# Building the expert gates of a two-layer trunk on one core: VectorE makes every one-hot part, and all gates pass through HBM

## The reference, cut to what matters

```python
def fourier_mix(u):                      # 4 groups of 256 channels, real part of a 2-D transform
    f = jnp.fft.fft2(ug, axes=(1, 3), norm='ortho').real

def peer_ffn(h, w_pq, sub_keys, peer_u, peer_v):
    q = (hf @ w_pq).reshape(T, PEER_HEADS, 2, PEER_KEY_DIM)
    s = jnp.einsum('thpd,hpnd->thpn', q, sub_keys)
    s1, i1 = lax.top_k(s[:, :, 0], PEER_TOPK)          # 16 of 128 first keys
    s2, i2 = lax.top_k(s[:, :, 1], PEER_TOPK)          # 16 of 128 second keys
    cand_s = s1[..., :, None] + s2[..., None, :]
    cand_i = i1[..., :, None] * PEER_KEYS + i2[..., None, :]
    top_s, pos = lax.top_k(cand_s, PEER_TOPK)          # 16 pairs per head and token
    gate = jax.nn.softmax(top_s, axis=-1)
    ...
    a = jnp.einsum('tkd,td->tk', ub, xb)               # ub: the chosen rows of peer_u
    a = jax.nn.gelu(a, approximate=False) * gb
    return jnp.einsum('tk,tkd->td', a, vb)             # vb: the chosen rows of peer_v
```

## Time and profile before

| what | before |
|---|---|
| median of 3 runs (lowest to highest) | 4188.33 us (4185.52 to 4189.72) |
| the profiled execution, its own time | 4193.56 us |
| its span, first to last instruction | 4191.4 us |
| busy share PE, PEld, DVE, ACT, POOL | 91%, 82%, 49%, 34%, 31% |
| mean granted TensorE clock | 0.937 |
| HBM read, written | 510.65 MB, 37.22 MB |

### The profile page before, as it was taken

One profiled execution on the slowest core, in us unless ns is written; L12 is line 12 of the kernel. 1 busy time (PEld: TensorE's weight loads), 2 busy tenths in 40 slices (PEclk: granted clock), 3 DMA queues, 4 the chain that ended last, 5 costly groups with the idle time before them and its releaser, 6 DMA issues.

```text
span 4191.4 us, 63927 instructions
## 1 busy us (share of the span) xinstructions
PE 3794.0 (91%) x20274; PEld 3456.9 (82%) x20274; DVE 2036.4 (49%) x3928; ACT 1409.3 (34%) x2015; POOL 1307.9 (31%) x585
## 2 busy tenths in 40 slices
PE   4999898966699999999989999998666999999998
PEld 4999798966678888898979987898666788888887
DVE  6586436965555222222246954479555632222223
ACT  2334323422233333333333342333222333333333
POOL 1332133543322222222213221345333222222222
PEclk8999999977789999999999999999677999999999
DMA  5486132322134444444436841333220444444442
GB/s 204 161 252 209 56 111 86 111 81 100 65 113 149 139 143 137 142 140 142 135 117 198 252 158 53 116 96 110 101 100 23 154 144 140 142 138 142 141 141 97
DMA packets 204743, 549.05 MB, mean 131 GB/s; under 512 B 17136, under 2 KB 87152, under 8 KB 202608
## 3 DMA queue, kind: packets, MB, share of 16 engines
q1 hardware_dynamic: 128016, 465.88, 34.3%
q10 hardware_dynamic: 76640, 82.06, 5.7%
HBM read 510.65 MB, written 37.22 MB: 131 GB/s over the span
## 4 chain that ended last, share of the span: by engine, by line
PE 83%; DVE 6%; issue 5%; POOL 2%; ACT 2%; DVEq 1%; DMA 0%; POOLq 0%; ACTq 0%; SPq 0%
PE bank L671 26%; PE bank L449 17%; PE bank L450 16%; PE bank L451 16%; PE bank L649 5%; DVE hot L1505 2%; POOL split_lo L360 1%; POOL hot L1112 1%; PE bank L542 1%; ACT split_hi L355 1%; PE bank L563 1%; PE bank L467 0%; PE bank L438 0%; PE bank L596 0%; DVE raw L376 0%
## 5 line engine op out<-in xcount | busy, mean ns | idle before, releaser
L360 POOL TENSOR_TENSOR split_lo<-raw,split_hi 128x1024 fp32r<-128x1024 f32 x436 | 1068.4, 2451 | 2637.3 <-ACT split_hi L355 2637.3
L449 PE MATMUL bank<-h_hi,split_hi 128*128 128x384 f32 x3712 | 1276.3, 344 | 84.9 <-DVE h_lo L1169 63.1
L355 ACT ACTIVATE split_hi<-raw 128x1024 fp32r<-128x1024 f32 x768 | 813.9, 1060 | 1490.4 <-PE bank L451 1202.8
L450 PE MATMUL bank<-h_lo,split_hi 128*128 128x384 f32 x3712 | 1259.7, 339 | 0.0
L451 PE MATMUL bank<-h_hi,split_lo 128*128 128x384 f32 x3712 | 1258.2, 339 | 0.0
L360 DVE TENSOR_TENSOR split_lo<-raw,split_hi 128x1024 fp32r<-128x1024 f32 x332 | 411.9, 1241 | 1341.9 <-ACT split_hi L355 1341.5
L449 PEld LDWEIGHTS bank<-h_hi,split_hi 128*128 128x128 f32 x3712 | 711.3, 192 | 121.0 <-DVE h_lo L1169 78.1
L450 PEld LDWEIGHTS bank<-h_lo,split_hi 128*128 128x128 f32 x3712 | 712.5, 192 | 7.8
L451 PEld LDWEIGHTS bank<-h_hi,split_lo 128*128 128x128 f32 x3712 | 710.2, 191 | 0.0
L671 PE MATMUL bank<-split_hi,a_hi 128*128 128x512 f32 x1536 | 490.8, 401 | 6.0 <-DVE a_lo L1530 5.8
L649 PE MATMUL bank<-hot,hot 128*128 128x128 bf16 x2304 | 284.5, 297 | 224.4 <-POOL hot L1112 131.4
(11 more groups left out here) (167 smaller groups left out, 2852.3 us busy)
## 6 DMA issues: line engine op xcount, KB each, us to landing
raw<-panels SPq DMA_DIRECT2D x768, 512.0 KB, 3.3
mod_raw<-mod_panels SPq DMA_DIRECT2D x96, 512.0 KB, 4.4
gates_spilled<-kept ACTq DMA_DIRECT2D x8, 4096.0 KB, 11.4
spilled<-gates_spilled ACTq DMA_DIRECT2D x128, 256.0 KB, 3.8
raw<-mod_panels SPq DMA_DIRECT2D x16, 512.0 KB, 4.5
bias<-bias_in ACTq DMA_DIRECT2D x16, 256.0 KB, 2.7
dft<-dft_in ACTq DMA_DIRECT2D x2, 1152.0 KB, 8.7
silu_c<-c_in ACTq DMA_DIRECT2D x2, 1024.0 KB, 5.1
```

What stands on the lines that cost most here:

```text
L355: nc.scalar.activation(col(split_hi, s % 2, D), col(raw, s, D), ACT.Copy).then_inc(hi_ready[s], 1)
L360: eng.tensor_tensor(col(split_lo, s % 2, D), col(raw, s, D), col(split_hi, s % 2, D).bitcast(F32), ALU.subtract).then_inc(lo_ready[s], 1)
L449: mm(out, w_hi, col(rhs_hi, kk, n), start=(kk == 0), stop=False)
L450: mm(out, w_hi, col(rhs_lo, kk, n), start=False, stop=False)
```

## The change

VectorE now makes everything for the gate matmuls, for one tile of 4 tokens at a time, in a ring of four buffers: `keys_hot` writes both one-hots with one instruction of 1024 elements, one tile ahead, and `gated_hot` all three gated parts with one of 1536. POOL has no work in the gate stage until its end; the `split_lo` of the panels there moves to DVE, one after each four tiles. The gate stage has 6 groups instead of 3: one score panel, then 4 tiles (16 tokens) instead of 8. One more group of 4 score panels (FINAL_G) runs behind it, so 52 score panels run ahead of the outputs instead of 36, and 52 output panels run in a row. A chunk is 32 tokens; all 12 chunks are stored to HBM, and the gates come back for four panels j at a time (12 x 128 x 128 values, 768 KB). DVE then gates a panel with one instruction. In the Fourier step the channel table keeps 129 cosine and 127 sine columns and two zero columns (258 instead of 512); the second half of the channels is taken from the same columns with the sine tables negated, and the rows of `w_four_out` are reordered on the host to match.

```diff
-BATCH = 2 * TILE_T
-NB = T // BATCH
-CHUNK_T = 64
+CHUNK_T = 32
-SPILLED = CHUNKS - KEPT
+HOTS = 4
+HOT = (2 + PARTS) * TILE_T * P
+BLOCK = 4
-ALONE_G, WITH_G = 6, 3
-EARLY_G = ALONE_G + WITH_G
+ALONE_G, WITH_G, FINAL_G = 6, 6, 1
+EARLY_G = ALONE_G + WITH_G + FINAL_G
...
-            def one_hots(n, b):
-                dve.wait_ge(gate_mm, l * NT + 2 * n + 2)
-                dve.wait_ge(hot1_pool, l * NB + n + 1)
...
+            def keys_hot(n, r):
+                dve.wait_ge(gate_mm, l * NT + n + 1)
+                shape = [P, 2, P, TILE_T]
+                V.tensor_tensor(hot_pair(r),
...
+                                ALU.is_equal).then_inc(eq_ready, 1)
+            def gated_hot(n, r):
+                dve.wait_ge(eq_ready, l * NT + n + 1)
+                shape = [P, PARTS, P, TILE_T]
+                V.tensor_tensor(hot_parts(r), hot_pair(r)[:, 0, :, :].unsqueeze(1).broadcast_to(shape),
...
+                                ALU.mult).then_inc(hot_ready, 1)
+            def hot_group(i, last=False):
+                for s in range(SLOTS):
+                    for r in range(PANEL_TILES):
+                        n = (i * SLOTS + s) * PANEL_TILES + r
+                        if not (last and s == SLOTS - 1 and r == PANEL_TILES - 1):
+                            keys_hot(n + 1, (r + 1) % HOTS)
+                        gated_hot(n, r)
+                    split_panel_lo(dve, *ahead(l * GROUPS + (FIRST["peer"] + ALONE_G) + i, s))
...
-            with pool.Fori(0, WITH_G) as i:
-                for s in range(SLOTS):
-                    split_panel_lo(pool, *ahead(peer + ALONE_G + i, s))
-                    for b in range(BATCHES):
-                        third_part((i * SLOTS + s) * BATCHES + b, b % 2)
+            for s in range(SLOTS):
+                split_panel_lo(pool, *ahead(peer + ALONE_G + WITH_G, s))
...
+            early_gelu(ALONE_G + WITH_G, 0)
+            early_gelu(ALONE_G + WITH_G, 1)
+            for b in range(KEPT):
+                act.wait_ge(gates_stored[b], (l + 1) * (CHUNKS // KEPT) * 16)
+            load_gates(0, 0)
+            load_gates(1, 1)
+            early_gelu(ALONE_G + WITH_G, 2)
+            early_gelu(ALONE_G + WITH_G, 3)
...
-                        last = mm(bank[4 + u % 2][:, :], col(f, 2 * g + c)[:, t * P:(t + 1) * P],
-                                  dft[:, DFT_CH + c * 512:DFT_CH + (c + 1) * 512], start=(c == 0), stop=(c == 1))
+                        last = mm(bank[4 + u % 2][:, 0:FC], col(f, 2 * g + c)[:, t * P:(t + 1) * P],
+                                  dft[:, DFT_CH + c * FC:DFT_CH + (c + 1) * FC], start=(c == 0), stop=(c == 1))
```

More of the change, by code:

```diff
@@ L554, in fourier_tokens @@
                     out = bank[6 + u % 2]
[L555 to L558, removed]
+                    cosines, sines = dt, HALF + 1 + dt
+                    for w0, which in ((cosines, 0), (sines, 1 + dt)):
+                        mm(out[:, 0:TP], yg[:, w0:w0 + P], dft[:, DFT_P + which * TP:DFT_P + (which + 1) * TP],
+                           start=(which == 0), stop=(which > 0))
                     for t in range(2):
-                        for part in range(2):
-                            w0 = (1 + t) * 512 + part * FD + dt * P
-                            r0 = DFT_S + (2 * t + part) * TS
+                        for w0, which in ((cosines, 0), (sines, 1 + dt)):
+                            w0 += (1 + t) * FC
+                            r0 = DFT_S + (3 * t + which) * TS
                             last = mm(out[:, TP:T], yg[:, w0:w0 + P], dft[:, r0:r0 + TS],
-                                      start=(t + part == 0), stop=(t + part == 2))
+                                      start=(t == 0 and which == 0), stop=(t == 1 and which > 0))
                     last.then_inc(y2_ready, 1)
@@ L634, in _, with build_gates @@
             route_tiles(TT - 1)
[L636 to L650, removed]
+            def build_gates(n, r):
+                pe.wait_ge(hot_ready, l * NT + n + 1)
+                pe.wait_ge(gate_copied, l * NT + n + 1)
+                keys2, parts = hot_pair(r), hot_parts(r)
+                for t in range(TILE_T):
+                    w = keys2[:, 1, :, t]
+                    o = col(bank[2 + r], t, P)
+                    for c in range(PARTS):
+                        last = mm(o, w, parts[:, c, :, t], start=(c == 0), stop=(c == PARTS - 1))
+                last.then_inc(gate_mm, 1)
             carry(pe)
@@ L996, in split_act, with pair @@
                 copy(col(a_hi, b), col(act_f, b)).then_inc(ahi_ready, 1)
-            def pair(i, p, load=True, last=False):
+            def pair(i, load=None, last=False):
                 g = peer + i
@@ L1005, in pair @@
                 split_act(2 * i + 1, 1, (g, 0))
-                if load:
-                    load_gates(i + 2, p)
+                if load is not None:
+                    load_gates(*load)
                 if not last:
@@ L1543, in _, with early_outputs @@
             carry(dve)
-            with dve.Fori(0, NB // 2) as i:
-                one_hots(2 * i, 0)
-                one_hots(2 * i + 1, 1)
-            def gated_early(i, s):
-                j = i * SLOTS + s
-                gated(j, s % 2, lambda at, n: gel_early[:, bass.ds(j * T + at, n)], s // 2, i)
-            def early_outputs(i, first=False):
+            keys_hot(0, 0)
+            with dve.Fori(0, WITH_G - 1) as i:
+                hot_group(i)
+            hot_group(WITH_G - 1, last=True)
+            def early_outputs(i, p, turn, first=False):
                 for s in range(SLOTS):
-                    gated_early(i, s)
+                    j = i * SLOTS + s
+                    gate_act(j, s % 2, s, gel_early[:, bass.ds(j * T, T)], p, turn)
                     if s % 2 == 0 and not (first and s == 0):
```

207 lines of the change are left out of this document (94 added, 113 removed).

## The result

The changed kernel takes 3926.83 us (median of 4 runs, 3925.07 to 3929.48) against 4188.06 us before (4185.52 to 4189.72): ratio 0.9377, 95% interval 0.9361 to 0.9394. The prediction was 3941 us, with 3905 to 4005 as its range. The profiled execution took 3925.07 us, its span is 3923.0 us, 268 us less than before. The medians lie 261 us apart; the profiled execution before was 5.5 us above its median.

The account below looks back on a forecast made before the run. PE bounds all long stretches except the gate stage, 305.4 us twice per launch, where it waits for POOL and DVE. 4193.56 - 228.4 (two layers) - 19 (Fourier) = 3946 us, 3941 with the median 5.2 us lower; range 3905 to 4005.

Parts of the forecast that it names:

- the clock term: Gate stage: panels lose a tenth of the 84 us that half clock would cost, 8 us per layer.
- First tile: Start of the gate stage: without POOL's split beside DVE, the first tile starts near 864.0 instead of 868.5 us.
- 24 periods: Gate stage: PE sets 24 periods of one panel and four tiles, 9.84 us each, less the first panel: 232.0 us.
- Rival A: Gate stage: the clock stays at half for the score panels, 84 us instead of 8 per layer, 4093 us; chance 0.09.
- Four last panels: End of the gate stage: four last score panels, each covered by POOL's split chain, take 17 us.
- Wait ahead of the outputs: From last score to first output: gelu, split, rounding and `a_lo` beside POOL's split make PE wait 4.3 us.
- Sixteen pair steps: Pairs: 16 pair steps of 8.40 us become output panels of 4.30 us in a row, 65.6 us less per layer.
- The Fourier term: Fourier step: 48 matmuls per layer shortened by 0.215 us each, 10.3 us; taken as 9.5, 19 us in all.
- C: Gate stage: hand-overs do not overlap, PE takes tiles at DVE's pace, period 11.5 us, 4021 us; chance 0.05.
- D: Gate stage: DVE's two-operand instructions keep their long form and bound it, period 22.4 us, 4546 us; chance 0.04.
- B: Gate stage: tile matmuls run faster once the clock is up, a tile taking 0.77 us, 3819 us; chance 0.04.

Follow-up runs that it names:

- x1_eight: Changed kernel with eight tiles behind each of 12 score panels instead of four behind each of 24, still 52 panels ahead of the outputs: 3930.70 us.
- x9_fewer_ahead: Changed kernel with eight tiles behind each of 12 score panels and 44 score panels ahead of the outputs instead of 52: 3925.53 us.
- x5_weights_flat: Changed kernel with the tile matmuls' weights read as 128 neighbouring elements instead of every fourth, giving other gates than the right ones: 3921.91 us.
- x6_both_flat: Changed kernel with tile matmuls' weights and gated parts both read as neighbouring elements, giving other gates than the right ones: 3821.14 us.
- x10_pairs: Changed kernel with gated parts laid out by token pairs, written in two instructions of 768 elements; TensorE's moving side steps 4 bytes, not 8: 3809.35 us.
- x3_pool_third: Changed kernel with only the third gate part of each tile back on POOL, the panels' splits staying on VectorE: 3931.96 us.

## Why the prediction was right

Every step held, and the forecast was 14 us high. The traces put it 21 us high, of which the clock term makes 16; every other term is off by 1.3 us a layer or less, steps 2 and 5 the other way. Seven of the 21 us came back by chance: the profiled execution after lies 1.8 us below its median, where I had counted with 5.2 us above.

1. *First tile.* 4.5 us per layer predicted, 5.3 found; the same three instructions, without POOL beside them.
2. *24 periods.* 232.0 predicted, 232.7 found. A panel with the hand-over behind it takes 4.28 us instead of 4.18, and four tiles 5.59 instead of 5.66, counted from first start to first start. The reading that PE would set the period, VectorE resting 2.5 us in it, held as it stands (2.77).
3. *Clock.* This term was the wrong size: 8 us were set aside, and none was lost in the periods: the granted clock is 0.99 over the stage and 1.00 from 862 to 1084 us. Rival A fell. By the rule that I cited from the Trainium skill (TensorE: Matmul & The Clock Gate, "A second HAM failure mode: psum-queue depth-cycling") a stage that goes round its PSUM banks with short idles would have swung between the two levels. This trace has the banks and the cycle without the idle time, and stays at 1.00 from period to period; x1_eight does so too.
4. *Four last panels.* 17 predicted, 16.8 found.
5. *Wait ahead of the outputs.* 4.3 predicted, 4.54 found, by the mechanism named.
6. *Sixteen pair steps.* 65.6 predicted, 66.9 found. The number is right and the step is still misleading: it reads as a gain of its own. The sixteen panels cost 12 x 4.28 + 16.8 = 68 us in steps 2 and 4, so the exchange is even, as x9_fewer_ahead shows. What paid was that PE no longer stands.

The Fourier term was taken a little under its upper end, 9.5 of 10.3; the trace gives 10.1. The loads from odd columns, which I could not price, cost nothing. Of the rivals, C (hand-overs that do not overlap) and D (long instructions on VectorE) are refuted by the rows of the period. B had the tile matmuls wrong in the same way as the forecast: both asked whether the clock sets their 0.118 us. It does not, and the weights hardly do (x5_weights_flat); x6_both_flat and x10_pairs show that the reading of the moving side did, so that over 100 us lay in a layout that the forecast took as given.

## What to carry to other kernels

When an engine's program has two jobs, look at which one stands in front: a job that waits for the slow chain delays a job that could have run, and moving the first away was worth 245 us in the changed kernel, while the speed of either was worth a few there. Count a panel that moves at both places before you call its removal a gain. And once TensorE sets a stage, ask of its matmuls how their operands lie in memory: time per matmul that does not follow the clock was a sign of it here.

## What the runs showed of the hardware

- 48 matmuls of 128 bf16 columns whose moving operand steps by 8 bytes take 5.84 us, 5.72 with flat weights, and at half the clock they stand no further apart. With a step of 4 bytes they take 3.28 us, 0.068 each; with no step on either side one takes 0.061 us. The Trainium skill (SBUF — State Buffer, "Door 1: The DMA port swizzle") says that accesses run at full rate as long as two of them fall into the same 16 bytes, which a step of 8 bytes does. For the moving operand the runs disagree: 4 bytes are nearly free, 8 are not.
- VectorE's key instruction, with two operands in SBUF, takes 1.11 us instead of 0.685 on the mean, and its split 2.03 instead of 1.22, where POOL multiplies 512 elements at a time beside it (x3_pool_third). The Trainium skill (SBUF — State Buffer, "Who interferes with whom") calls the port pair that the two share an exclusive lock. The trace agrees: the keys that begin at 965.51 us, 0.34 us behind POOL's instruction, end 0.54 us behind its end. In x3_pool_third these waits cost some 5 us in all, about what the runs can tell from none, since VectorE is not the bound there.
